# Requests for the last two GLU weight columns, tied to DVE's progress in the fifth column

## The reference

```python
u = _rmsnorm(h, g_mix)
proj = jnp.einsum('ntd,de->nte', u, w_in)          # nine column groups of 1024
a_b, a_c, a_h, a_z, b_v, b_g, b_z, gate_a, gate_b = jnp.split(proj, SPLITS, axis=-1)
...
v = b_v * jax.nn.sigmoid(b_g)                      # the GLU
ext_b = jnp.concatenate([buf_b.astype(v.dtype), v], axis=1)
c = _causal_dwconv(ext_b, w_conv_b) + b_conv_b
yb = jax.nn.silu(_layernorm(c, ln_g, ln_b)) * jax.nn.silu(b_z)
```

## Time and profile before

| | |
|---|---|
| time, median of 3 runs | 885.43 us (883.58 to 886.11) |
| time of the profiled execution | 885.41 us |
| longest core span in it | 882.6 us (core 3) |
| spans of cores 0 to 7 | 879.6, 882.4, 879.2, 882.6, 877.8, 881.3, 878.1, 881.4 us |
| PE busy on the page's core | 854.6 us, 97% of the span |
| DVE, ACT, POOL busy | 509.0, 301.9, 146.1 us |
| share of the DMA engines' time, queue q0 (POOL's) and q1 (SP's) | 25.3% and 24.9% |

### The profile page before, as it was taken

How to read it: one execution, slowest core, us unless ns; L and a number is a source line. 1 busy time by engine, 2 the same in 40 slices (tenths; PEclk the granted TensorE clock), 3 DMA queues, 4 the chain that set the end, 5 groups by cost and what they waited for, 6 DMA issues and landing times.

```text
span 882.4 us, 15282 instructions; the slowest of 8 cores (877.8 to 882.6 us)
## 1 busy us (share of the span) xinstructions
PE 854.6 (97%) x4970; PEld 441.6 (50%) x4970; DVE 509.0 (58%) x794; ACT 301.9 (34%) x568; POOL 146.1 (17%) x275
## 2 busy tenths in 40 slices
PE   7999999999999999999999999999999999999993
PEld 4886555555454444454454544444444444444441
DVE  2455234576997777777677732333233325777775
ACT  4773224355443232423323321111111112444443
POOL 3242101100101101020110101110001001344442
PEclk9999999999999999999999999999999999999997
DMA  9987899996203213030413276522222145766642
GB/s 190 258 154 98 160 184 176 151 155 116 49 1 48 38 24 61 13 61 1 61 15 59 33 147 96 86 38 46 49 49 33 22 83 129 196 182 170 172 127 98
DMA packets 94108, 84.42 MB, mean 96 GB/s; under 512 B 53296, under 2 KB 74800, under 8 KB 93488
## 3 DMA queue, kind: packets, MB, share of 16 engines
q0 software_dynamic: 27776, 31.17, 25.3%
q1 hardware_dynamic: 66256, 52.29, 24.9%
HBM read 86.80 MB, written 15.61 MB: 116 GB/s over the span
## 4 chain that ended last, share of the span: by engine, by line
PE 85%; DMA 7%; issue 2%; DVE 2%; ACT 2%; POOL 1%; DVEq 0%; POOLq 0%; SPq 0%; ACTq 0%
PE ps L409 65%; PE ps L849 7%; PE ps L870 6%; PE ps L604 4%; DMA t_v<-vd 3%; DMA t_x<-x 2%; PE ps L876 1%; DMA vd<-t_vrow 1%; PE ps L672 1%; DMA t_ring<-w_in 1%; ACT t_xb L424 1%; ACT t_xb L484 1%; DVE t_tmp L714 1%; PE ps L498 0%; PE ps L919 0%
## 5 line engine op out<-in xcount | busy, mean ns | idle before, releaser
L409 PE MATMUL ps<-t_uT,t_ring 128*128 128x512 bf16 (+2 forms) x3200 | 542.6, 329 | 1.5 <-DMA t_ring<-w_in 0.7
L409 PEld LDWEIGHTS ps<-t_uT,t_ring 128*128 128x128 bf16 x3200 | 278.2, 98 | 253.5 <-issue 4.3
L823 DVE TENSOR_TENSOR t_tmp<-ps,t_tmp 128x512 f32<-128x512 f32 (+1 forms) x80 | 48.7, 611 | 151.2 <-PE ps L409 150.6
L343 POOL DMA_DIRECT2D t_ring<-w_in x72 | 39.0, 543 | 391.2 <-PE ps L409 388.3
L820 ACT ACTIVATE t_tmp<-ps 128x512 f32<-128x512 f32 (+1 forms) x80 | 42.3, 532 | 177.2 <-PE ps L409 177.2
L781 ACT ACTIVATE t_tmp<-t_tmp,t_vid 128x512 f32<-128x512 f32 (+1 forms) x40 | 30.0, 749 | 124.0 <-DVE t_tmp L778 124.0
L535 DVE TENSOR_TENSOR t_vrow<-ps,t_tmp 128x512 bf16<-128x512 f32 (+2 forms) x52 | 25.2, 485 | 80.8 <-PE ps L409 38.1
L409 PE MATMUL ps<-t_cb,t_ring 128*128 128x512 bf16 (+1 forms) x320 | 65.4, 347 | 0.0
L409 PE MATMUL ps<-t_yaT,t_ring 128*128 128x512 bf16 (+1 forms) x320 | 65.4, 347 | 0.0
L849 PE MATMUL ps<-t_wo_t,t_cb 128*128 128x512 bf16 x272 | 61.5, 379 | 0.0
L870 PE MATMUL ps<-t_wpg_t,t_u2T 128*128 128x512 bf16 x240 | 54.3, 379 | 0.0
(11 more groups left out here) (99 smaller groups left out, 764.1 us busy)
## 6 DMA issues: line engine op xcount, KB each, us to landing
t_ring<-w_in POOLq DMA_DIRECT2D x72, 256.0 KB, 6.5
t_x<-x SPq DMA_DIRECT2D x17, 512.0 KB, 8.8
t_xs<-x SPq DMA_DIRECT2D x17, 512.0 KB, 4.7
t_cb<-t_c SPq DMA_DIRECT2D x64, 128.0 KB, 5.1
y<-t_yt SPq DMA_DIRECT2D x15, 512.0 KB, 3.2
vd<-t_vrow SPq DMA_DIRECT2D x28, 128.0 KB, 5.4
t_v<-vd SPq DMA_DIRECT2D x7, 512.0 KB, 7.0
t_ring<-w_oa POOLq DMA_DIRECT2D x8, 256.0 KB, 8.0
```

The lines of the kernel that those rows point to most:

```text
L343: S.add("pool", lambda e: e.dma_start(out=out, in_=in_), reads=reads, writes=list(writes) + [swq()], dma=key)
L409: S.add("pe", lambda e, k=k: e.matmul(ps[:, b, 0:n], lhsT=ring[k_ring][:, k, :], rhs=rhs_fn(k), start=(k == 0), stop=(k == NCH - 1)), read ...
L823: S.add("dve", lambda e, p=p, t=t: e.tensor_tensor(out=tmp[t][:, 0:n], in0=ps[:, p, 0:n], in1=tmp[t][:, 0:n], op=ALU.mult), reads=[f"ps{p} ...
```

## The change

`pump` takes a list of resources that its requests read, and `wdone` can give its buffers back without a request. At the end of chunk 3 of columns 0 and 1 the weights of columns 4 and 5 are requested as before. At the end of chunk 3 of columns 2 and 3 nothing is requested any more. The four tiles of columns 6 and 7 are requested in column 4 instead: two behind job (4, 1), with a wait for DVE's product of that job, and two behind job (4, 3), with a wait for DVE's product of that one. The resource `done{j}_{si}` is written by the product so that a request can read it.

```diff
-        def pump(maxn=8):
+        def pump(maxn=8, reads=()):
...
-                pdma(ring[k].rearrange("p k m -> p (k m)"), WL[t][0], [], [f"ring{k}"], f"ring{k}")
+                pdma(ring[k].rearrange("p k m -> p (k m)"), WL[t][0], reads, [f"ring{k}"], f"ring{k}")
...
-        def wdone(g):
+        def wdone(g, refill=True):
             for t in WG[g]:
                 ring_free.append(slot_of[t])
-            pump()
+            if refill:
+                pump()
...
-                      reads=[f"ps{bv}", f"tmp{tg}"], writes=[f"vst{q}"])
+                      reads=[f"ps{bv}", f"tmp{tg}"], writes=[f"vst{q}", f"done{j}_{si}"])
...
-                    wdone(s2w[j][0])
+                    wdone(s2w[j][0], j < 2)
...
             s2_proj(j, si)
+            if j == 4 and si in (1, 3):
+
+                pump(2, [f"done4_{si}"])
             if si == 3:
                 wdone(s2w[j][0])
```

## The result

The changed kernel takes 892.16 us, the median of 12 runs (890.19 to 893.48). Against the kernel before on the same chip the ratio is 1.0067, with a 95% interval of 1.0057 to 1.0078: 6 us slower, where 884.5 us and no change were forecast and 887.8 us was the end of the range. The ratio compares fast runs alone: three of the 12 of the kernel before on that chip were slow ones (948.6 to 1053.4 us). The profiled execution took 892.07 us, its longest core span is 890.3 us; that of before was 882.6 us.

A forecast was written before the change was run, and what follows sets the result against it. PE, 97% busy, was taken to lose time only to column waits and lowered clock. With the wait before half 0 gone and other terms zero, the slowest core fell 0.9 us to 881.7: 884.5 us, range 882.8 to 886.5 (8 in 10: 881.9 to 887.8).

The forecast's parts named there:

- What bounds the kernel: PE, busy 97% of the span; only its waits or clock loss matter, and DMAs cost the slowest core 3.5 us.
- the two waits: PE's waits for read-back columns: first before half 0 (0.88 to 2.31 us), second before half 4 (1.82 to 2.93 us).
- W1 goes: Wait before half 0 vanishes: 0.88 us on core 3, 1.45 on core 1, 2.31 + 1.59 on core 7.
- The new waits cost nothing: Weight requests waiting for DVE's products of jobs (4, 1) and (4, 3) delay nothing needed: zero.
- Part 3, the first pair: Two tiles requested at 97 us, moving in 97 to 105 when DMA engines are little busy: zero.
- Part 3, the second pair: Two tiles requested at 111 us beside column 2's load; wait before half 4 changes by -2.6 to +3.8 us, taken as 0.
- The slower rival: Half 4: tiles served ahead of column 2's load add up to 3.8 us, 888.3 us in all; chance 0.15.
- The faster rival: Half 4: column 2's load starts on an emptier queue, its wait shrinks; 882.7 us, or 881.9 without it; chance 0.27.

The follow-up runs named there:

- the second experiment: Changed kernel with only two tiles requested behind job (4, 3), the other two behind job (5, 1): ratio 1.0046 to the kernel before, 887.61 us.
- the fifth experiment: Changed kernel with column 7's pair back at the fourth column's end, only column 8's pair behind job (4, 3): ratio 1.0010 to the kernel before, 884.99 us.

## Why the prediction was wrong, point by point

*What bounds the kernel*, and the two waits: right. In the kernel with requests one by one, which has neither wait, the longest span is 880.3 us, against the 879.1 us reckoned for core 1 without waits. Two readings beside it were wrong and changed nothing: core 0 had the first wait too (1.75 us), and core 7 was spared the second not because it came late to half 4, for its request was as early before it as on the other cores (10.6 us), but because its load took 10.3 us, the shortest of the eight.

*W1 goes*: right on all eight cores. Column 0's load lands after 4.8 to 6.1 us; the reckoning had 7.4 to 9.5 us, since it let POOL's four remaining tiles share their time with the load.

*The new waits cost nothing*: right as far as PE goes. No core waits for a tile in columns 6 and 7.

*Part 3, the first pair: wrong, and the step that failed.* "In 96 to 100 the DMA engines are busy for 31% of the time only the earlier trace rows, and column 1's load has left by then, so I take zero." The pair is requested at 97.8 but moves from 100 to 105. The row read ends where that begins; the next stretch, on the same core 3 of the kernel before, reads:

```profile
100.00:105.00 5.00, 5.00 (x29) 2.65 (x27) 0.79 (x3) 1.28 (x3) 0.00 (x0) 1.00 1.04 242
```

The share there is 1.04, all of it SP's queue: column 1's load until 103.3, which the change does move away, and the transfers to `cb`, which the prediction never costed, since PE doesn't wait for them. Their place in line is ahead of column 2's load. The size of the term: with no tile near column 2's load it takes 8.6 to 10.2 us with the first pair and 7.0 to 9.1 us without; with four tiles near, 15.1 to 17.7 us on seven of eight cores against 6.5 to 8.3.

*Part 3, the second pair: wrong in its reason.* "It is never dry in column 2's flight, so that two tiles more make it longer, and mostly delay what stands behind them in POOL's own queue." It took 0 for a term that came to 4.1 to 6.5 us of landing time on seven cores. Service in turn was read as an equal share of time. The counts show about equal numbers of packets while the tiles run, so that the share of time goes by what a packet costs: 0.20 us for a tile's. Then every tile that is in front of the load's last packets costs it most of its 1.9 us; two tiles less there were worth about 4 us in the second experiment. The Trainium skill ("DMA: Bandwidth & Descriptors", "Queues, rings and completion order") says that an engine takes the queues in turn, packet by packet; the traces agree with that as far as 138 and 139 or 146 and 125 packets in 2 us go, though not for packets of 64 bytes (692 beside 188), and the prediction drew the wrong conclusion from it, that depth doesn't matter. Depth matters as long as the other queue's transfer has more packets left than the tiles have.

*The slower rival* named the place and the mechanism, tiles served ahead of column 2's load, priced it at 3.8 us and gave it 0.15. Its place is right. Its size was short: the load takes 4.1 to 6.5 us longer on seven cores, a request that is late by 3 us on core 6 and by up to 1.1 us on the others comes on top, and so do 1.4 to 2.7 us of lower clock. And it took the second pair alone to be enough, which the fifth experiment refutes.

*The faster rival* may have been right in its mechanism, but that isn't shown. With the first pair away from 97 us and the other tiles behind column 2's load, that load takes 5.8 to 9.5 us; but there the two tiles that had stood ahead of it are gone too, and this alone brought it to 7.0 to 9.1 us with column 1's load still requested between 95.0 and 98.2 us. What is shown is that the change put its first pair into the place it had just cleared.

What stays open: how much of the late requests comes from SP's own issue time and how much from its queue being full (the rows show requests that take 5.4 us instead of 2.6 for four, not why); what decides on which cores column 2's load is hit; and why the odd cores had more waiting than the even ones in the profile of before.

## What to carry to other kernels

A prefetch that is moved to a stretch where the DMA engines are idle must be followed to when it moves, not to when it is requested, and what stands in the other queue then must be costed even if no engine waits for it: it may be in line ahead of something that one does wait for. Large transfers near a load of small packets that PE waits for did best here when requested one at a time, 6 to 9 us apart; two or four in a row made the next such load late or slow, wherever they were put, even when they had landed before it was requested. When two halves of a change each look free, try them apart: here one half alone was free, and the other made both dear.

## What the runs showed of the hardware

- Beside weight tiles (2 KB a packet) packets of POOL's and SP's queues were served about one for one (146 and 125, 138 and 139 in 2 us), and SP's queue fell to 14 to 15% of the engines' time. With packets of 64 bytes on SP's queue it was 692 to 188.
- The four transfers to `cb` near 98 and 105 us took SP 2.9 and 2.6 us to issue on core 0 and 5.4 and 3.7 us on core 6 of one execution; the store behind column 2's load took it 7.0 us on core 6.
- A load of 1024 packets of 512 bytes took 3.9 us at best, 5.8 to 10.2 us in traffic without tiles ahead, and 15.1 to 17.7 us on seven cores with four tiles that moved before it was through.
- After waits of 4.98 to 8.32 us PE's next 20 matmuls took 4.4 to 5.8 us instead of 3.02, in part at the lower clock (granted 0.50), and the job behind them ran at full speed again (3.62 to 3.78 us for its 16 matmuls).
